# Leading the second attention with its memory heads, spreading its head transposes, preloading three activation tables, and moving late values and first output terms of the latent attention

## The chip, the cores and the metric

The kernel runs on one core of one Trainium2 chip. The metric is the device time of one execution in microseconds (us). PE is the tensor engine, ACT the scalar engine, DVE the vector engine, POOL the engine that issues some of the transfers, SP the queue that issues the weight transfers. All matrices are float32, and one product of the program is two matmul instructions in the trace (128x512: x2).

## The reference, cut to what matters

Two blocks of layers on one sequence of 256 tokens, width 1024. The change touches the second attention of the first block ("fgt") and the only latent attention of the second block ("mla"), with the start of the mixture of experts behind it.

```python
# first block, second layer: 12 heads with forgetting, 4 memory heads
s = einsum('bthd,bshd->bhts', q, k) * scale + dcum_t - dcum_s     # causal
o_mix = softmax(s) @ v
o_mem = softmax(q_mem @ k_mem.T * scale) @ v_mem                   # memory_attention
x = x + concat([o_mix, o_mem]) @ w_o
# second block, first layer: 8 heads over 512 keys (context and latent)
kv = rms_norm(c_kv) @ w_ukv                                        # keys and values
y_lat = softmax(q_l @ k_all.T * scale) @ v_all @ w_o
x = x + g1 * y_lat
# then: route each token to 2 of 32 experts; silu(x @ w_gate) * (x @ w_up) @ w_down
```

## The kernel before, in words

Each engine runs its own program, written out by hand, and waits on semaphores; the order on an engine is the order of its code. Signals are kept in stages (`st["headsB"]`, `st["fgt"]`, `st["mlaU"]`, ...); `after(engine, "fgt")` waits for all signals of a stage. PSUM has 8 banks of 128x512. Weights come through a ring of six slots (`take`, `used`), filled by SP.

The second attention. `heads("headsB", ...)` turns 56 blocks of 128 tokens so that head width lies on partitions, four blocks to a bank: memory queries (in two halves of 64 columns each, so two instructions a block), memory keys, then queries and keys of the 12 forgetting heads with 66 rows. `evac("headsB", 14)` copies the banks out, the even ones by ACT, the odd ones by DVE. Only when all are copied (`after(..., "headsB")`) does `attention("fgt")` begin, on all three engines. It runs over units, one head each: `i` goes from 0 to 18 for 16 units. In iteration `i` PE makes the scores of unit `i` (for memory heads, which are `paired`, those of `i` and `i+1` together), then `outputs(i-3)` (one group of two heads at a time), then `probs_T(i-2)` (3 or 4 transposes of the probabilities), then a `fill`, one product of the output projection `wo1` that already has its heads. DVE finds the maximum (as a minimum of the negated scores), ACT the exponential, DVE the division; ACT and DVE share the copies of transposed probabilities. The units are the 12 forgetting heads, then the 4 memory heads. `out_gemm` then makes the rest of `wo1`.

The latent attention. Before it, PE makes keys (`uk`, 8 products of two halves) and values (`uv`, 8 groups of 2 products, each waiting for the key copy of its bank); ACT scales the values into `vN`; then `attention("mla")` runs over 16 units (8 heads by 2 tiles of tokens). Beside it, `row_pair` makes rows that the next stage needs. After it, `entry` makes the output projection (`product(c, h)`, 8 products each), adds it to the tokens and prepares the routing; `route` picks experts, and `experts` runs 16 rounds of three blocks of 32 rows each. SP's `load_experts` fetches the first two experts when ring slots come free, the third after `mla_o`, and the others after `route`, each when a quarter counter of the rounds allows.

ACT loads a table when a function of another set comes: exponential after root or logarithm, silu after exponential.

Of the kernel before, what the change touches and what calls it, by code (L numbers as in the profile page):

```python
# [11 lines left out]
P = 128  # L12
KT = D // P
# [170 lines left out]
def two_blocks(nc, dram, out_x):  # L184
# [5 lines left out]
    with ctx:  # L190
# [19 lines left out]
        sum_q = sb("sum_q", [P, TC])  # L210
        gx, fgcol, gsm = (sb(n, [P, KT]) for n in ("gx", "fgcol", "gsm"))
# [128 lines left out]
        projB = area(0, TC, NH + NM, AUG)  # L340
        kvS = area(TC * (NH + NM) * AUG, TC, 2 * NH, AUG)
# [175 lines left out]
        def mla_units():  # L517

            units = []
            for h in range(MH):  # L520
# [18 lines left out]
        for i in range(12):  # L539
            FILL["fgt"][6 + i] = (i // 2, i // 2, i % 2)  # L540
# [3 lines left out]
        CONV_BANKS = 6  # L544

# [110 lines left out]
        def col(t, c, c0, n=2 * HD):  # L656
# [6 lines left out]
        HEADS_B = [(projB[:, c, NH + 2 * j, 0:HD], projB[:, c, NH + 2 * j + 1, 0:HD]) for j in range(NM // 2)  # L663
                   for c in range(TC)] + mem_k
# [3 lines left out]
        ROWS_B = [P] * 2 + [AUG] * 12  # L668

# [19 lines left out]
        def heads_out(rows, scaled):  # L689

            def at(i):
                n = rows[i]
                return (headsT[0:n, 4 * i:4 * i + 4, :], ps[0:n, i % BANKS, :].rearrange("p (a b) -> p a b", a=4),
                        -SCALE_A if i in scaled else 1.0)
            return at
# [4 lines left out]
        def shared_out(i):  # L700
            w, c = i // TC, i % TC
            if w < 3:
# [7 lines left out]
               "headsB": heads_out(ROWS_B, (0, 2, 3, 4, 5, 6, 7)),  # L710
# [141 lines left out]
        def _(pe):  # L852
# [119 lines left out]
            def heads(name, blocks, rows, after_two=None, bank0=0):  # L972

                s = st[name]
                for i in range(len(blocks) // 4):
                    bank_free(s, i)
                    if i == 2 and after_two is not None:
                        after(pe, after_two)
                    for j in range(4):
# [14 lines left out]
            def attention(name, o_name=None, beside={}):  # L994
# [4 lines left out]
                if o_name is not None:  # L999
                    order = [k for _, k, h in FILL[name].values() if h == 0]  # L1000
                    w = out_chunks(order[0], KT - 1 if KT - 1 not in order else order[-1])
# [48 lines left out]
                for i in range(n + LAG + 1):  # L1050
# [4 lines left out]
                    if name == "mla" and i in ROWS_AT:  # L1055
                        j = ROWS_AT.index(i)
                        if j:
                            g = st["g1_0"]["gate_copied"]
                            pe.wait_ge(g.sem, g.at(2 * j))
                        row_pair("g1_0", j, 6)  # L1060
# [103 lines left out]
            def entry(o_name, lhs, tag):  # L1164
                s, e, r = st[o_name], st["ent" + tag], st["route" + tag]
                w = [take().rearrange("p (k n) -> p k n", k=KT) for _ in range(2)]

                def product(c, h, between=None):
# [1970 lines left out]
```

## Time and profile before

| | before |
|---|---|
| median of 3 runs (lowest, highest) | 2126.44 us (2125.73, 2127.97) |
| the profiled execution | 2125.36 us |
| its span in the trace | 2123.5 us |
| PE busy | 1984.4 us, 93% |
| granted TensorE clock, mean | 0.978 |

The span is the profiled execution less 1.9 us around it. Times in the rows below are from the start of the span. The clock is a share of full speed: 1.00 is 2.4 GHz, 0.50 is 1.2 GHz. In brackets behind a row of the timeline stands the time the engine was idle before it and what ended that.

### The profile page before, as it was taken

The numbers are of one execution on the slowest core, as the hardware profiler recorded it, in microseconds if no ns is written. First come the engines' busy times: TensorE is split into PE (matmuls) and PEld (weight loads), VectorE is DVE, ScalarE is ACT, GpSimd is POOL, SyncE is SP. The second block draws the span as 40 slices with busy tenths as digits, with TensorE's granted clock in tenths as the row PEclk, the third lists the DMA queues.
The fourth block names the chain that finished last, engine by engine and source line by source line (L and its number), as shares of the span: only waits on it lengthen the run. The fifth ranks groups of instructions, "written<-read, shape, count | busy, mean of one in ns | idle before, by whom it ended". The sixth has DMA issues, their size and how long they took to land.

```text
span 2123.5 us, 29332 instructions
## 1 busy us (share of the span) xinstructions
PE 1984.4 (93%) x9625; PEld 1080.3 (51%) x9626; DVE 992.9 (47%) x2203; ACT 682.4 (32%) x1092; POOL 45.0 (2%) x80
## 2 busy tenths in 40 slices
PE   8999999999999999999999888889998999888887
PEld 4536777646577775554433333334774333333333
DVE  2566886303398543444444333335224444333335
ACT  1451000103400003142555444444103554444444
POOL 2000000000000000000000000001000000000000
PEclk9999999998999999999999999999999999999999
DMA  9507995433289443305899999999555999999996
GB/s 306 210 7 290 362 346 220 159 119 140 106 343 366 149 165 136 122 37 201 351 414 422 419 416 422 423 423 367 218 198 210 400 419 423 422 423 422 422 422 256
DMA packets 78655, 619.89 MB, mean 292 GB/s; under 512 B 9664, under 2 KB 10000, under 8 KB 15712
## 3 DMA queue, kind: packets, MB, share of 16 engines
q1 hardware_dynamic: 67968, 540.51, 63.4%
q0 software_dynamic: 6944, 66.35, 8.2%
q10 hardware_dynamic: 3648, 11.89, 1.4%
q8 instruction: 44, 0.72, 0.1%
q14 instruction: 51, 0.42, 0.1%
HBM read 605.08 MB, written 13.63 MB: 291 GB/s over the span
## 4 chain that ended last, share of the span: by engine, by line
PE 68%; DMA 24%; DVE 3%; ACT 2%; issue 1%; DVEq 0%; SPq 0%; ACTq 0%; POOL 0%; POOLq 0%
PE ps L856 26%; DMA big<-in_w_up 21%; PE ps L1277 14%; PE ps L1103 14%; PE ps L1115 7%; PE ps L870 2%; PE ps L1250 2%; PE ps L1279 2%; DMA big<-in_w_gate 1%; DMA big<-in_w_down 1%; ACT big L1780 1%; PE ps L1261 1%; DMA big<-in_first_final_g 0%; DMA big<-in_dense 0%; PE ps L1125 0%
## 5 line engine op out<-in xcount | busy, mean ns | idle before, releaser
L1277 PE MATMUL ps<-big,hT 128*32 128x512 f32 x3072 | 698.2, 608 | 81.8 <-ACT big L1780 66.8
L1279 PE MATMUL ps<-big,hT 128*32 x1536 | 697.0, 608 | 0.0
L1780 ACT COPY big<-big 128x1024 f32 x384 | 395.6, 1046 | 494.2 <-PE ps L1279 269.6
L2538 DVE TENSOR_SCALAR big<-big 128x1024 f32 x384 | 262.1, 692 | 437.4 <-PE ps L1279 301.7
L1277 PEld LDWEIGHTS ps<-big,hT 128*32 128x32 f32 x3072 | 189.0, 111 | 459.9 <-issue 254.3
L1103 PE MATMUL ps<-hT,big 128*128 128x256 f32 x1408 | 311.2, 379 | 0.0
L856 PE MATMUL ps<-big,hT 128*128 128x512 f32 (+4 forms) x784 | 302.1, 537 | 3.4 <-ACT hT L1719 2.1
L1103 PEld LDWEIGHTS ps<-hT,big 128*128 128x128 f32 x1408 | 266.7, 190 | 49.4 <-issue 15.2
L856 PEld LDWEIGHTS ps<-big,hT 128*128 128x128 f32 x784 | 139.2, 192 | 131.7 <-issue 123.4
L1279 PEld LDWEIGHTS ps<-big,hT 128*32 128x32 f32 x1536 | 158.3, 111 | 3.7
L1115 PE MATMUL ps<-big 128*128 128x512 f32 x352 | 159.3, 595 | 0.7 <-DVE big L2302 0.7
L856 PE MATMUL ps<-big 128*128 128x512 f32 (+15 forms) x636 | 141.0, 451 | 13.8 <-issue 5.3
L2312 DVE SCALAR_TENSOR_TENSOR big<-big,s_ccol 128x512 f32<-128x512 f32 x196 | 147.4, 752 | 7.0
L1744 ACT ACTIVATE big<-big 128x256 f32<-128x256 f32 x44 | 18.3, 417 | 367.3 <-DVE big L2294 367.3
L1250 PE MATMUL ps<-big,hT 128*96 128x512 f32 x256 | 118.1, 604 | 1.2 <-DVE hT L2504 1.2
L856 PE MATMUL ps<-hT,big 128*128 128x256 f32 (+1 forms) x480 | 113.2, 397 | 1.9 <-ACT hT L2021 1.9
L856 PEld LDWEIGHTS ps<-big 128*128 128x128 f32 (+8 forms) x636 | 69.7, 176 | 79.8 <-issue 64.3
L856 PEld LDWEIGHTS ps<-hT,big 128*128 128x128 f32 x480 | 92.3, 193 | 23.7 <-issue 11.9
L1115 PEld LDWEIGHTS ps<-big 128*128 128x128 f32 x352 | 66.1, 190 | 73.5 <-issue 69.0
L2276 DVE TENSOR_TENSOR big<-ps,big 128x512 f32<-128x512 f32 x44 | 30.4, 690 | 115.4 <-PE ps L1103 114.6
L1250 PEld LDWEIGHTS ps<-big,hT 128*96 128x96 f32 x256 | 39.3, 163 | 78.0 <-issue 76.7
L2572 DVE TENSOR_TENSOR hT<-hT,ps 96x512 f32<-96x512 f32 x32 | 21.9, 683 | 88.6 <-PE ps L1279 88.6
(331 smaller groups left out, 1258.9 us busy)
## 6 DMA issues: line engine op xcount, KB each, us to landing
big<-in_w_gate SPq DMA_DIRECT2D x128, 1024.0 KB, 23.7
big<-in_w_up SPq DMA_DIRECT2D x128, 1024.0 KB, 23.2
big<-in_w_down SPq DMA_DIRECT2D x128, 1024.0 KB, 21.7
big<-in_dense SPq DMA_DIRECT2D x52, 1536.0 KB, 8.7
big<-in_dense POOLq DMA_DIRECT2D x28, 2048.0 KB, 9.9
big<-in_dense SPq DMA_DIRECT2D x20, 2048.0 KB, 7.9
y_rows<-c_res ACTq DMA_DIRECT2D x30, 384.0 KB, 7.0
big<-in_dense SPq DMA_DIRECT2D x7, 1024.0 KB, 31.7
```

Of the source, the lines that this page charges most:

```text
L856: ins = nc.tensor.matmul(out, lhsT, rhs, start=start, stop=stop)
L870: ins = nc.tensor.transpose(out, rows, const["ident"][0:k, 0:k])
L1103: ins = nc.tensor.matmul(ps[:, t % 2, f * S:(f + 1) * S], w[:, k, f * P:(f + 1) * P], hT[:, k, S:2 * S], start=k == 0, stop=k == KT - 1)
L1115: ins = nc.tensor.matmul(ps[:, 4 + 2 * c + h, :], gT[:, t % 2, c * P:(c + 1) * P], w[:, h * BW:(h + 1) * BW], start=t == 0, stop=t == FT - 1)
L1250: ins = nc.tensor.matmul(ps[0:ROWS, h, :], onehot[:, t, :], fN[:, t, h * BW:(h + 1) * BW], start=t == 0, stop=t == T - 1)
L1277: nc.tensor.matmul(ps[g * SLOTS:(g + 1) * SLOTS, bank, :], xT[:, k, g * SLOTS:(g + 1) * SLOTS], side[:, g - 1, quarter % 2, at:at + BW], s ...
L1279: return nc.tensor.matmul(ps[0:SLOTS, bank, :], xT[:, k, 0:SLOTS], experts3[:, bass.ds(here, 1), kind * CH + row:kind * CH + row + BW] .re ...
L1780: nc.scalar.copy(side[:, 1, quarter % 2, :], experts3[:, bass.ds(there, 1), lo:lo + QW] .rearrange("p a n -> p (a n)")).then_inc(s["side2_ ...
L2276: tt(U[:, par, :, 2:S + 2], ps[:, par, :].rearrange("p (a b) -> p a b", a=2), token_scale, mult)\
L2312: ins = stt(acc, mod_w[j % 2][:, k, :], ccols[:, k, col:col + 1], acc, mult, add)
L2538: ts(side[:, 0, quarter % 2, :], experts3[:, bass.ds(there, 1), lo:lo + QW].rearrange("p a n -> p (a n)"), 1.0, None, mult).then_inc(s["si ...
L2572: tt(hm[0:ROWS, :], sgm[0:ROWS, :], ps[0:ROWS, 3, :], mult).then_inc(s["hidden_done"].sem, 1)
```

## The change

1. The second attention has its 4 memory heads first (units 0 to 3), then the 12 forgetting heads. The memory queries are kept in a packed piece `mem_q`, so that a block is turned by one instruction; for this ACT and DVE write the third and fourth bank of `b_in` in two instructions each instead of one.
2. Of the 14 banks of head transposes only the first two (memory queries and keys) are done ahead of the attention, in banks 3 and 4. The other 12 are done two at a time in iterations 0 to 5, in banks 6 and 7, queries and keys of two heads; their copies stand in the same iterations on ACT and DVE.
3. The 12 products of `wo1` in the attention stand in iterations 7 to 18 instead of 6 to 17, in the order of heads that are ready.
4. ACT runs a one-column activation (`table_for`) where a table is needed later: exponential before the first and the second attention, silu in `route`.
5. In the latent attention the values of the last four heads (4 groups) are made by PE in iteration 0, behind the first pair of scores, and scaled by ACT in iteration 1. Two products of the output projection are made in iterations 15 and 17; the wait for the end of the attention stands ahead of the last product of `product(0, 0)` instead of ahead of the first.

```diff
+        mem_q = [area((c * (NH + NM) + NH) * AUG, MEM_W) for c in range(TC)]
-               "fgt": forget_units() + mem_units(NH, F_QM, F_KM), "mla": mla_units()}
-        SLOT0 = {"nsa": 2, "fgt": 0, "mla": 0}
+               "fgt": mem_units(2, F_QM, F_KM) + forget_units(), "mla": mla_units()}
+        SLOT0 = {"nsa": 2, "fgt": 2, "mla": 0}
-            FILL["fgt"][6 + i] = (i // 2, i // 2, i % 2)
+            FILL["fgt"][7 + i] = (i // 2, (6, 7, 0, 1, 2, 3)[i // 2], i % 2)
+        V_BANKS = ((3, 4, 5, 6), (7, 3, 4, 5))
+        FIRST_BANK = {"0": 7, "1": 0}
+        TURNS_B = [0, 1] + [x for i in range(6) for x in (2 + i, 8 + i)]
+        TURN_BANK_B = [3, 4] + [6, 7] * 6
...
+            def copied_B(i):
+                e = st["headsB"]["dve_evac" if i % 2 else "act_evac"]
+                pe.wait_ge(e.sem, e.at(i // 2 + 1))
+            def turn_B(i):
+                g, bank = TURNS_B[i], TURN_BANK_B[i]
+                if i >= 4:
+                    copied_B(i - 2)
+                for j in range(4):
+                    tr(ps[0:ROWS_B[g], bank, j * P:(j + 1) * P], HEADS_B[4 * g + j],
+                       st["headsB"]["banks_ready"].sem if j == 3 else None)
...
-            heads("headsB", HEADS_B, ROWS_B, after_two="dcum")
-            after(pe, "headsB")
-            w = attention("fgt", "wo1")
+            for i in range(2):
+                turn_B(i)
+            after(pe, "dcum")
+            for i in range(2):
+                copied_B(i)
+            steps = {i: [lambda i=i: turn_B(2 * i + 2), lambda i=i: turn_B(2 * i + 3)] for i in range(6)}
+            for i in (3, 5):
+                steps[i] += [lambda i=i: copied_B(i - 1), lambda i=i: copied_B(i)]
+            steps[6] = [lambda: after(pe, "headsB")]
+            w = attention("fgt", "wo1", steps)
...
+            def late_values():
+                for c in range(4):
+                    if c:
+                        pe.wait_ge(u["uv_scaled"].sem, u["uv_scaled"].at(c))
+                    values(c, 1)
+                used()
+            for c in range(4):
+                pe.wait_ge(u["uk_scaled"].sem, u["uk_scaled"].at(c + 3))
+                values(c, 0)
+            pe.wait_ge(u["uk_scaled"].sem, u["uk_scaled"].end)
...
-            after(pe, "mlaU")
-            attention("mla")
-            after(pe, "mla")
+            attention("mla", beside={0: [late_values], 15: [lambda: early_out(0)], 17: [lambda: early_out(1)]})
+            out_done = st["mla"]["out_done"]
...
+            def table_for(function):
+                nc.scalar.activation(warm[:], const["ident"][:, 0:1], function)
...
                 nc.scalar.activation(ee, ae, ACT.Exp).then_inc(s["route_act"].sem, 1)
+                table_for(ACT.Silu)
...
             evac("mem1", TC)
-            evac("headsB", 14)
+            evac("headsB", 2)
+            attention("fgt", {i: [lambda i=i: evac("headsB", 2 * i + 4, 2 * i + 2)] for i in range(6)})
             after(act, "headsB")
-            attention("fgt")
```

PE at the head of the second attention, before: `128x128` out of `c_ident` are transposes of 128 rows, `66x128` those of the forgetting heads, the others scores.

```order
L870 MATMUL ps<-c_ident,big 64x128
L856 MATMUL ps<-c_ident,big 64x128
L870 MATMUL ps<-c_ident,big 128x128 x4
L870 MATMUL ps<-c_ident,big 66x128 x48
L856 MATMUL ps<-big 128x128
L856 MATMUL ps<-big 128x256
L856 MATMUL ps<-big 128x128
L856 MATMUL ps<-big 128x256
L856 MATMUL ps<-big 128x128
L856 MATMUL ps<-big 128x256
L870 MATMUL ps<-c_ident,big 128x128 x3
```

The same place now.

```order
L877 MATMUL ps<-c_ident,big 128x128 x8
L863 MATMUL ps<-big 128x256 x4
L877 MATMUL ps<-c_ident,big 66x128 x16
L863 MATMUL ps<-big 128x256 x4
L877 MATMUL ps<-c_ident,big 128x128 x4
L877 MATMUL ps<-c_ident,big 66x128 x8
L877 MATMUL ps<-c_ident,big 128x128 x4
L877 MATMUL ps<-c_ident,big 66x128 x8
L863 MATMUL ps<-big 128x128
L863 MATMUL ps<-big 128x256
L863 MATMUL ps<-big 64x256 x4
```

The 48 transposes of the forgetting heads stand between scores and transposes of probabilities of the memory heads, and the eight instructions on halves are gone.

ACT at the same place, before: `big<-ps 66x512` are copies of turned heads, `big,psums` the exponentials.

```order
L1937 ACT_TABLE_LOAD
L1937 ACTIVATE big<-big 128x24
L1654 ACTIVATE big<-ps,rstd_m 128x512
L1654 ACTIVATE big<-ps 128x512
L1654 ACTIVATE big<-ps 66x512 x6
L1706 ACT_TABLE_LOAD
L1706 ACTIVATE big,psums<-big,mx 128x128
```

ACT now.

```order
L1998 ACT_TABLE_LOAD
L1998 ACTIVATE big<-big 128x24
L1699 ACT_TABLE_LOAD
L1699 ACTIVATE warm<-c_ident 128x1
L1707 ACTIVATE big<-ps,rstd_m 128x512
L1707 ACTIVATE big<-ps 128x512
L1759 ACTIVATE big,psums<-ps,mx 128x256 x2
L1707 ACTIVATE big<-ps 66x512
L1759 ACTIVATE big,psums<-ps,mx 128x256 x2
L1707 ACTIVATE big<-ps 66x512
L1759 ACTIVATE big,psums<-ps,mx 128x256 x2
L1779 COPY big<-ps 128x512
```

The table load stands ahead of the copy of the memory product, and each of the six copies of turned heads stands behind an exponential.

PE from the values into the latent attention, before: `big,hT 128x512 x16` are the 8 value groups, `big 128x512` scores, `hT,c_ones` the first `row_pair`.

```order
L856 MATMUL ps<-hT,big 128x512 x16
L856 MATMUL ps<-big,hT 128x512 x16
L856 MATMUL ps<-big 128x512 x8
L856 MATMUL ps<-hT,c_ones 128x512 x2
L870 MATMUL ps<-c_ident,big 128x128 x8
```

The same place now.

```order
L863 MATMUL ps<-big,hT 128x512 x8
L863 MATMUL ps<-big 128x512 x4
L863 MATMUL ps<-big,hT 128x512 x8
L863 MATMUL ps<-big 128x512 x4
L863 MATMUL ps<-hT,c_ones 128x512 x2
```

Four value groups stand behind the first pair of scores instead of ahead of it.

PE at the end of the latent attention, before: `big 128x256` are outputs, `big,hT 128x512 x8` is `product(0, 0)` of the output projection, `128x36` the row that the routing needs.

```order
L870 MATMUL ps<-c_ident,big 128x128 x8
L856 MATMUL ps<-big 128x256 x4
L870 MATMUL ps<-c_ident,big 128x128 x8
L856 MATMUL ps<-big 128x256 x4
L856 MATMUL ps<-big,hT 128x512 x8
L856 MATMUL ps<-big,c_ones 128x36
```

The same place now.

```order
L863 MATMUL ps<-big,hT 128x512
L863 MATMUL ps<-big 128x256 x4
L877 MATMUL ps<-c_ident,big 128x128 x8
L863 MATMUL ps<-big,hT 128x512
L863 MATMUL ps<-big 128x256 x4
L863 MATMUL ps<-big,hT 128x512 x6
L863 MATMUL ps<-big,c_ones 128x36
```

Two of the eight products of the first output bank stand one ahead of each of the last two outputs.

## Rows read from the trace of the kernel before

**Rows 1.** The page, the chain that ended last: shares of the span by engine

```profile
PE 68%; DMA 24%; DVE 3%; ACT 2%; issue 1%; DVEq 0%; SPq 0%; ACTq 0%; POOL 0%; POOLq 0%
```

**Rows 2.** Windows at the first expert round: busy by engine, clock, DMA share, GB/s

```profile
1010.00:1015.00 5.00, 5.00 (x32) 2.57 (x27) 1.66 (x4) 2.03 (x2) 0.00 (x0) 0.80 0.11 18
1020.00:1025.00 5.00, 4.28 (x30) 1.80 (x24) 0.69 (x1) 2.27 (x3) 0.00 (x0) 1.00 1.01 426
```

**Rows 3.** Timeline of SP: first transfer of the fourth expert

```profile
1013.92 5.20 SPq L781 DMA_DIRECT2D big<-in_w_gate  x4
```

**Rows 4.** Chain in order of time, expert rounds: start, us, what

```profile
1127.29 23.77 DMA big<-in_w_up
```

**Rows 5.** Timeline of PE, head transposes and second attention: start, us, [idle before]

```profile
502.01 0.27 PE L870 MATMUL ps<-c_ident,big 128*64 128x128 f32 x1 [0.58 <-DVE big L2057]
...
504.35 5.89 PE L870 MATMUL ps<-c_ident,big 128*128 128x128 f32 x52
511.18 2.20 PE L856 MATMUL ps<-big 66*128 66x128 f32 x12 [0.94 <-ACT big L1654]
516.11 0.90 PE L870 MATMUL ps<-c_ident,big 128*128 128x128 f32 x3 [2.73 <-DVE big L2218]
...
553.84 10.54 PE L856 MATMUL ps<-big,hT 128*128 128x512 f32 x24 [0.56 <-ACT hT L1719]
```

**Rows 6.** Windows in the second attention, columns as in Rows 2

```profile
508.00:510.00 2.00, 2.00 (x21) 1.97 (x19) 1.63 (x3) 1.35 (x3) 0.00 (x0) 1.00 0.00 0
...
514.00:516.00 2.00, 0.00 (x0) 0.00 (x0) 0.66 (x4) 1.99 (x9) 0.00 (x0) 0.50 0.00 0
...
524.00:526.00 2.00, 1.15 (x9) 0.78 (x9) 1.96 (x11) 0.99 (x4) 0.00 (x0) 1.00 0.00 0
```

**Rows 7.** Chain in order of time, second attention in its even flow

```profile
530.61 0.87 PE ps L856 x8
531.48 0.48 PE ps L870 x3
531.95 1.52 PE ps L856 x6
```

**Rows 8.** Timeline of ACT, second attention

```profile
509.84 0.59 ACT L1654 ACTIVATE big<-ps 66x512 f32<-66x512 f32 x1 [0.28 <-PE ps L870]
512.99 1.28 ACT L1706 ACT_TABLE_LOAD   x1 [2.56 <-DVE mx L2201]
```

**Rows 9.** Timeline of DVE, second attention: copy of turned heads

```profile
510.28 0.69 DVE L2057 TENSOR_SCALAR big<-ps 66x512 f32<-66x512 f32 x1 [0.19 <-PE ps L870]
```

**Rows 10.** Timeline of ACT, first attention: exponential of a memory head's first half

```profile
89.02 0.47 ACT L1706 ACTIVATE big<-ps,mx 128x256 f32<-128x256 f32 x1
```

**Rows 11.** Timeline of DVE, first attention: maximum, reciprocal, division

```profile
90.63 0.68 DVE L2206 TENSOR_REDUCE mx<-ps 128x2 f32<-128x512 f32 x1
91.23 0.16 DVE L2214 RECIPROCAL pinv<-psums 128x2 f32<-128x2 f32 x1
91.42 0.62 DVE L2218 TENSOR_SCALAR big<-big,pinv 128x256 f32<-128x256 f32 x2
```

**Rows 12.** Timeline of PE, latent attention

```profile
884.67 13.90 PE L856 MATMUL ps<-big,hT 128*128 128x512 f32 x32
899.44 3.01 PE L856 MATMUL ps<-big 128*128 128x512 f32 x8 [0.87 <-ACT big L2003]
904.11 3.04 PE L856 MATMUL ps<-big 128*128 128x512 f32 x8 [1.66 <-ACT big L1706]
...
947.66 1.97 PE L856 MATMUL ps<-big 128*128 128x256 f32 x8 [0.83 <-ACT big L1726]
...
954.16 7.11 PE L856 MATMUL ps<-big,hT 128*128 128x512 f32 x16 [0.87 <-ACT hT L1719]
```

**Rows 13.** Timeline of DVE behind the latent attention: sum for the routing

```profile
958.76 0.66 DVE L2365 TENSOR_REDUCE big<-big 128x36 f32<-128x288 f32 x1
```

**Rows 14.** Timeline of PE, first expert round

```profile
1021.47 0.62 PE L1277 MATMUL ps<-big,hT 128*32 128x512 f32 x2 [0.72 <-ACT big L1780]
```

More of the change, by code:

```diff
@@ L970, in out_gemm, with heads @@
                 turn_of(1, 1)
-            def heads(name, blocks, rows, after_two=None, bank0=0):
+            def heads(name, blocks, rows):
                 s = st[name]
@@ L1000, in attention @@
                     order = [k for _, k, h in FILL[name].values() if h == 0]
-                    w = out_chunks(order[0], KT - 1 if KT - 1 not in order else order[-1])
+                    w = out_chunks(order[0], ([order[-1]] + [k for k in range(KT) if k not in order])[-1])
                 def fill(i):
@@ L1059, in attention @@
                             pe.wait_ge(g.sem, g.at(2 * j))
+                        else:
+                            e = st["mlaU"]["uv_scaled"]
+                            pe.wait_ge(e.sem, e.end)
                         row_pair("g1_0", j, 6)
@@ L1162, in row_pair, with entry, product @@
                     mm(ps[:, bank + h, :], const["ones"][:], d[:, 4 * h:4 * h + 4, :], True, True, s["gate_ready"].sem)
-            def entry(o_name, lhs, tag):
+            def entry(o_name, lhs, tag, w=None, begun=0, done=None):
                 s, e, r = st[o_name], st["ent" + tag], st["route" + tag]
-                w = [take().rearrange("p (k n) -> p k n", k=KT) for _ in range(2)]
-                def product(c, h, between=None):
-                    for k in range(KT):
+                if w is None:
+                    w = [take().rearrange("p (k n) -> p k n", k=KT) for _ in range(2)]
+                def product(c, h, between=None, begun=0):
+                    for k in range(begun, KT):
                         if between is not None and k == 4:
                             between()
-                        mm(ps[:, 2 * c + h, :], lhs(k, c), w[h][:, k, :], k == 0, k == KT - 1,
+                        if begun and k == KT - 1:
+                            pe.wait_ge(done.sem, done.end)
+                        mm(ps[:, FIRST_BANK[tag] if not c and not h else 2 * c + h, :], lhs(k, c), w[h][:, k, :], k == 0, k == KT - 1,
                            s["banks_ready"].sem if k == KT - 1 else None)
@@ L1646, in _, with evac @@
                     .then_inc(ident_loaded if name == "ident" else first_loaded, 16)
-            def evac(name, n):
+            def table_for(function):
+                nc.scalar.activation(warm[:], const["ident"][:, 0:1], function)
+            def evac(name, n, first=0):
                 s = st[name]
-                for i in range(0, n, 2):
+                for i in range(first, n, 2):
                     dst, src, factor = OUT[name](i)
@@ L1879, in _ @@
                 ins.then_inc(s["gelu_done"].sem, 1)
+            table_for(ACT.Exp)
             after(act, "mem0", "ropeA")
@@ L1999, in _, with values @@
             nc.scalar.copy(rkvB, ps[:, 0, :]).then_inc(q["scales_copied"].sem, 1)
-            for i in range(8):
-                c, h = i // 2, i % 2
-                act.wait_ge(u["uv_ready"].sem, u["uv_ready"].at(i + 1))
-                nc.scalar.activation(vN[:, c, h * BW:(h + 1) * BW], ps[:, (1 + i) % BANKS, :], ACT.Copy,
-                                     scale=rstd_kv[:, c:c + 1]).then_inc(u["uv_scaled"].sem, 1)
-            attention("mla")
+            def values(h):
+                for c in range(4):
+                    act.wait_ge(u["uv_ready"].sem, u["uv_ready"].at(4 * h + c + 1))
+                    nc.scalar.activation(vN[:, c, h * BW:(h + 1) * BW], ps[:, V_BANKS[h][c], :], ACT.Copy,
+                                         scale=rstd_kv[:, c:c + 1]).then_inc(u["uv_scaled"].sem, 1)
+            values(0)
+            attention("mla", {1: [lambda: values(1)]})
             after(act, "mla")
@@ L2774, in _ @@
             nc.vector.tensor_copy(kS[:, :, :, HD + 1], dc).then_inc(s["dcum_dve"].sem, 1)
-            evac("headsB", 14)
+            evac("headsB", 2)
+            attention("fgt", {i: [lambda i=i: evac("headsB", 2 * i + 4, 2 * i + 2)] for i in range(6)})
             after(v, "headsB")
-            attention("fgt")
             after(v, "fgt")
```

58 lines of the change are left out of this document (35 added, 23 removed).

## The prediction

> **What bounds the kernel now.** The chain that ended last is PE for 68% and DMA for 24% [rows 1]. Following it in order of time shows where each rules: PE down to the first expert round, then from about 1127 us on transfers of expert weights of 23 to 27 us, one round after the other [rows 4], and the same in the second set of experts. So the question for any gain ahead of the experts is whether the train of transfers starts earlier too. In the windows at the first round the transfer engines are nearly empty (share 0.11) just before the fourth expert's first transfer is issued at 1013.92, and full (426 GB/s) behind it [rows 2, 3]. That transfer waits for the routing and for the first quarters of round 0, both PE's. What PE gains before 1014 us is therefore passed on whole; what it gains inside the rounds meets a full train and is mostly lost.
>
> Next the timeline of PE where the change lies, reading the idle time in brackets. In the second attention, PE starts on the heads at 502.01; has 52 transposes in 5.89 us, 0.11 each; waits 0.94 for the last copies; makes scores from 511.18 to about 513.4; then waits 2.73 until 516.11, and the output projection's last part starts at 553.84 [rows 5]. The windows show what this wait brings: the clock is 1.00 through the transposes, 0.50 at 514 to 516, and 1.00 again at 524 [rows 6]. So PE ran at 1.2 GHz for some 10 us and was busy in it from 516.1 on: about 7.9 us that would be 4 us at 2.4 GHz.
>
> **The second attention, walked through.** Prices, all at full clock: four transposes 0.45 [rows 5]; in the even flow outputs of a pair of heads 0.87, three transposes 0.33 to 0.48, a fill with one unit's scores 1.52 [rows 7], of which the fill is 0.87 (24 instructions in 10.54, two a product [rows 5]), so scores 0.65; a pair of heads with fills 4.77 (the same outputs return at 535.38). ACT: copy of turned heads 0.59 [rows 8], exponential of a memory head two halves of 0.47 [rows 10]. DVE: maximum 0.68, reciprocal and division together about 0.75 [rows 11], copy of turned heads 0.69 [rows 9]. Scores of a pair of memory heads I take as 0.87, like the outputs, being four products on halves of the rows.
>
> PE from 502.01: 8 transposes to 502.9; it waits for both copies, DVE's last, to 503.8. Scores of units 0 and 1 to 504.7, 8 transposes to 505.6. Bank 6 comes free only when ACT has done exponential 0 (from DVE's maximum at 505.5, 0.92) and then the copy, 507.1: **a new stall of 1.5**. Behind the waiting transposes on PE are the next scores. Transposes to 508.0, scores of 2 and 3, transposes of probabilities, 8 transposes: 510.2. Then 0.15 for the division, and 0.95 for ACT's copy behind exponential 2 and a copy of probabilities: 511.75. From here DVE sets the pace. It has 0.68 + 0.75 + 0.69 an iteration and every other one a copy of probabilities of 0.69, 2.1 to 2.8 us, against PE's 2 to 3. I get the last head copies at 519.05, iteration 7's end at 521.65, four pairs of 4.77 to 540.8, and the tail of two outputs, three fills, seven transposes, 5.0, to 545.8. The output projection's last part starts at 545.8 instead of 553.84: **8.0 us less**. In it are the table load of 1.28 [rows 8], now in an idle stretch of ACT near 488 (costs nothing: the next ACT work is at 494), the four blocks turned in halves (2.4 us from 502.01 to 504.4, now 0.45), the 10 us from 504.4 in which nothing but transposes ran and then waited, the half clock, and the 0.56 ahead of 553.84, which the last fill covers.
>
> That is with the clock at 1.00 throughout. New gaps of 0.9, 1.5 and 1.1 us stand in the first 10 us, with little but transposes between. If it falls there once, for as long as before (10 us), PE does 5 us of full-clock work where the walk has 7.5 in that stretch; with a wait or two more that is 3 lost, 5.0 gained. Rows for both exist: in rows 6 the clock holds through transposes and falls in a wait of 2.73. I take 6.5, half-way, since no row decides it.
>
> The Trainium skill, "TensorE: Matmul & The Clock Gate", Part 4 (PE-mode transpose), says transposes do not count as PE being busy in the same way. The row of 508 to 510 us, nothing but transposes and clock 1.00, speaks against it. By the row the sum stays; by the rule the new head of the attention is cold from its start, which is the rival A below. The skill, "ScalarE: Activation LUTs", What ACT_TABLE_LOAD costs, gives about 2.66 us for a switch with a drain; here the load takes 1.28, ends at 514.27 [rows 8], and ACT is busy for 1.99 of the 2.00 us from 514 on [rows 6]: no drain. By the rule the sum would be 1.4 us better.
>
> **The first attention's table load** gives nothing. It stands at 87.72, but the division that needs exponential 0 starts at 91.23, behind DVE's own queue [rows 11]; 1.28 less on ACT ends there.
>
> **b_in in two instructions**: two more on ACT and on DVE, about 0.2 us each, under products of 6.9 us. Nothing.
>
> **Latent attention, start.** The 8 value groups take 13.90, 1.72 each; then stalls of 0.87 (ACT's last scaling) and 1.66 (exponential) [rows 12]. Now the four late groups, 6.9 us, stand between the first and second pair of scores, where the maximum and exponential cost PE 1.66. ACT scales a group in 0.7, so PE never waits for it, and the last is done 0.9 us after PE's, under 3.0 us of scores, ahead of the new wait at the row pair. **2.5 less.**
>
> **Latent attention, end.** Stalls of 0.83 before each of the last two outputs are filled by an early product of 0.87 each; their time is unchanged, but 1.7 us less is left behind. The stall of 0.87 ahead of 954.16 [rows 12] goes as well. PE would be done with `product(0, 0)` at about 958.3 instead of 961.1. What is late next is the routing row: DVE's sum ends at 959.42 [rows 13], and that hangs on transfers issued at the attention's end, which has not moved. So PE goes on at 959.5: **1.6 less**, not 2.6. Moving `used()` for the value weights delays one transfer by 3 us, of an expert used 100 us later: nothing.
>
> **Silu in `route`.** The load of 1.28 in round 0 makes PE wait 0.72 [rows 14], behind the train's start. 0 by the train, 0.7 in each of two layers if it counts; nearer to 0, as the transfer engines are full: 0.4 for both.
>
> Sum: 6.5 + 2.5 + 1.6 + 0.4 = 11.0. The profiled execution took 2125.36, so 2114.4; the median lies 1.1 above it: **2115.4**.
>
> **Rivals.**
> A. The clock stays low from 503 until the heads are turned. PE's work from 502.9 to the end of iteration 7 is 12 times 0.45 for heads, 0.87 twice and 0.65 four times for scores, 0.87 twice for outputs, 2.4 for probabilities and a fill of 0.87: 14.8 us at full clock, 29.5 at half. That is 532.4 instead of 521.65, so the second attention is 2.7 slower than before where the walk had 8.0 less; with the other 4.5, 2124.6. Low for half as long again as before, 2119 to 2121. For it: the gaps early, and short bursts; against it: rows 6 at 508, and that the clock came back in the kernel before after 10 us of which 8 were busy. 15% for 2118.5 to 2122.2, 5% beyond.
> B. It does not get through: the expert train has its own start. Then 2125 to 2126. Against it rows 2 and 3. 3%.
> C. Slower than before. The same clock, low on past the heads: each pair of heads then costs 4.77 more. With 1.8 left of the gain by rival A's end, it takes 1.8 + 4.3 = 6.1, more than one pair, to be 0.2% slower: low until about 544 us, 41 us in one go. Nothing in the rows of this stretch shows more than 10. 3%, at 2132 if it is low for three pairs.
> D. Better: the clock never falls there and the half clock behind the routing goes too. All of 8.0 + 2.5 + 1.6 + 1.4 is 13.5, 2113; below 2110 only with another clock gain. 4% below 2110.
>
> My forecast's own case, 2110 to 2118.5, has 70%. With rival A's nearer part the range 2110 to 2121 leaves out 4% below, 4% of rival A's nearer part and 11% beyond: 19%. A measurement of this kernel tells 0.2%, 4.3 us, from no change. Faster is all below 2122.2: 0.70 + 0.15 + 0.04 = 0.89; same takes rival A's end and B: 0.08; slower: 0.03.
>
> **What would show it.** After: the time from the first head transpose to the output projection's last part is 44 to 47 us instead of 51.8; the first exponential has no table load before it; the largest PE gap there is about 1.5, for ACT's copy behind the first exponential. PE's two stalls at the latent attention's start are gone; at its end a stall of about 1 us stands ahead of the 128x36 product, waiting for DVE. The fourth expert's transfer is issued about 11 us earlier, and the expert rounds keep their length. Wrong it would be if the clock falls at 503 to 507 and stays, if DVE's iterations take over 3 us, or if the train of transfers does not move.

## The result, and the profile after

The changed kernel takes 2115.05 us (median of 4 runs, 2111.78 to 2116.16) against 2126.96 (median of 4, 2125.73 to 2127.97): ratio 0.995, 95% interval 0.9935 to 0.9965. In a second set of runs it was 2114.79 against 2125.13, ratio 0.9946 (0.9933 to 0.996). The predicted time was 2115.4. The profiled execution took 2116.16, 9.2 less than that of before. The terms behind the sum are less well hit than the sum, as the rows and the experiments show. One run of the lead-only kernel below, 2159.07 us at a mean clock of 0.935, was in a slower state and is left out of its median and ratio.

The chain that ended last, by engine; against [rows 1], PE has two points more, the transfers one less.

```profile
PE 70%; DMA 23%; DVE 3%; ACT 2%; issue 2%; DVEq 0%; SPq 0%; POOL 0%; ACTq 0%; POOLq 0%
```

The timeline of PE through the second attention of the changed kernel: start, us, what, and in brackets the idle time before.

```profile
503.74 1.06 PE L877 MATMUL ps<-c_ident,big 128*128 128x128 f32 x8 [0.58 <-DVE big L2122]
505.89 1.14 PE L863 MATMUL ps<-big 64*128 64x256 f32 x8 [1.09 <-DVE big L2122]
506.95 1.06 PE L877 MATMUL ps<-c_ident,big 128*66 128x128 f32 x8
509.30 1.07 PE L877 MATMUL ps<-c_ident,big 128*66 128x128 f32 x8 [1.28 <-ACT big L1707]
...
514.22 1.07 PE L877 MATMUL ps<-c_ident,big 128*66 128x128 f32 x8 [0.63 <-ACT big L1707]
...
544.36 0.87 PE L863 MATMUL ps<-big 128*64 128x256 f32 x8 [0.72 <-issue]
...
548.49 3.70 PE L863 MATMUL ps<-big,hT 128*128 128x512 f32 x8
```

The last part of the output projection starts at 549.35, one product of 0.86 behind 548.49. I call the time from the first head transpose to there the stretch: 45.61 us, where [rows 5] give 51.83. The largest gap is 1.28, for ACT's copy behind the first exponential; 1.5 was forecast. The windows of [rows 6] now read:

```profile
508.00:510.00 2.00, 0.72 (x8) 0.70 (x8) 1.91 (x5) 1.87 (x8) 0.00 (x0) 1.00 0.16 68
514.00:516.00 2.00, 1.78 (x14) 1.45 (x16) 1.97 (x6) 1.66 (x6) 0.00 (x0) 1.00 0.00 0
524.00:526.00 2.00, 1.94 (x14) 1.13 (x12) 1.85 (x12) 1.08 (x5) 0.00 (x0) 1.00 0.00 0
```

The clock is 1.00 throughout, with PE busy for only 0.72 of 2.00 us in the first of them. The latent attention, against [rows 12] and [rows 13]:

```profile
881.32 7.03 PE L863 MATMUL ps<-big,hT 128*128 128x512 f32 x16
888.19 2.94 PE L863 MATMUL ps<-big 128*128 128x512 f32 x8
891.06 7.13 PE L863 MATMUL ps<-big,hT 128*128 128x512 f32 x16
898.03 2.94 PE L863 MATMUL ps<-big 128*128 128x512 f32 x8
...
946.95 5.31 PE L863 MATMUL ps<-big,hT 128*128 128x512 f32 x12
953.25 0.41 PE L863 MATMUL ps<-big,c_ones 128*128 128x36 f32 x2 [0.99 <-DVE big L2430]
```

Both stalls at its start are gone, and at its end the wait for DVE's routing row stands where it was forecast. The fourth expert's first transfer and the chain behind it, against [rows 3] and [rows 4]:

```profile
1005.58 6.14 SPq L788 DMA_DIRECT2D big<-in_w_gate  x4
```

```profile
1118.27 24.37 DMA big<-in_w_up
```

The transfer is issued 8.34 earlier, not 11 (9.69 in the second profile of the changed kernel). The account of this pair of profiles: 1.71 lost at the very start of the program, 6.22 gained in the stretch, 1.69 from there to the latent attention's first transposes of probabilities, 1.57 to the end of its output rows, 0.59 in the routing and first round. The 1.71 is a slower pass through the first products (last section), and 1 us is missing from the 1.69 for a stretch of half clock near 810 us. Between the first transfers of the two expert sets 2.36 is lost again, and behind the second set's 3.22 is gained, which makes 9.2. Over all profiles here the time between these two transfers runs from 627.1 to 631.5 us, of which the silu's early load accounts for only about 1. So a single pair can't tell terms of 1 or 2 us; the landmarks of each stage can.

### The profile page after: what moved, and what is told of

The parts are those of the page before. It is cut to its first block, busy times and chain, and to the rows that moved or that the text cites. A ratio compares the mean times of both kernels' runs of the same rounds, so it can differ in the third digit from the quotient of the medians.

```text
span 2114.3 us, 29316 instructions
## 1 busy us (share of the span) xinstructions
PE 1985.9 (94%) x9617; PEld 1080.2 (51%) x9618; DVE 992.3 (47%) x2204; ACT 682.9 (32%) x1097; POOL 45.7 (2%) x80
## 4 chain that ended last, share of the span: by engine, by line
PE 70%; DMA 23%; DVE 3%; ACT 2%; issue 2%; DVEq 0%; SPq 0%; POOL 0%; ACTq 0%; POOLq 0%
PE ps L863 26%; DMA big<-in_w_up 20%; PE ps L1302 15%; PE ps L1125 14%; PE ps L1137 7%; PE ps L877 2%; PE ps L1304 2%; PE ps L1275 2%; DMA big<-in_w_gate 1%; ACT big L1833 1%; PE ps L1286 1%; DMA big<-in_first_final_g 0%; DMA big<-in_w_down 0%; DMA big<-in_dense 0%; PE ps L1147 0%
## 5 line engine op out<-in xcount | busy, mean ns | idle before, releaser
L863 PE MATMUL ps<-big 128*128 128x512 f32 (+15 forms) x636 | 135.7, 438 | 9.5 <-issue 5.2
## 6 DMA issues: line engine op xcount, KB each, us to landing
big<-in_dense POOLq DMA_DIRECT2D x28, 2048.0 KB, 10.2
```

What stands on the lines that cost most here:

```text
L863: ins = nc.tensor.matmul(out, lhsT, rhs, start=start, stop=stop)
```

## The experiments

The table gives median and ratio to the kernel before (95% interval), from 5 rounds each (3 for the last; the first two rows are the runs of the result), and from each kernel's profile the stretch, how long the clock was 0.50 in it, and two landmarks of the latent attention: L1 from the end of the stretch to its first transposes of probabilities, L2 from there to the first transposes of the output rows. The half-clock times are read from windows of 1 us: one with a clock of 0.85 holds 0.3 us at 0.50. There is one profile of each row. The ratios are to runs of the kernel before in the same set, and not to the 2126.96: the medians of these were 2126.76 for the rows attention only, latent only and the two on the exponential, 2127.33 for lead only, products in the wait, no silu preload and two waits moved, 2125.13 for changed again, products among transposes and silu preload only, 2127.64 for the last.

| kernel | us | ratio | stretch | at 0.50 | L1 | L2 |
|---|---|---|---|---|---|---|
| before (profile above) | 2126.96 | | 51.83 | 10.2 | 355.06 | 59.30 |
| changed | 2115.05 | 0.995 (0.9935, 0.9965) | 45.61 | 0 | 353.37 | 57.73 |
| changed, again | 2114.79 | 0.9946 (0.9933, 0.996) | 45.61 | 0 | 353.40 | 57.84 |
| attention only | 2117.68 | 0.9962 (0.9948, 0.9975) | 45.61 | 0 | 355.35 | 59.30 |
| latent only | 2122.07 | 0.9975 (0.9962, 0.9987) | 54.03 | 17.1 | 352.16 | 57.70 |
| changed, no exponential preload | 2114.27 | 0.9947 (0.993, 0.9963) | 45.62 | 0 | 352.19 | 57.96 |
| before, exponential preload only | 2125.77 | 0.9995 (0.9983, 1.0007) | 51.81 | 13.7 | 355.15 | 59.30 |
| lead only | 2117.99 | 0.9966 (0.9954, 0.9979) | 49.40 | 3.4 | 352.51 | 57.79 |
| products in the wait | 2121.70 | 0.9976 (0.9964, 0.9988) | 50.55 | 3.4 | 354.89 | 59.30 |
| changed, no silu preload | 2117.02 | 0.9958 (0.9944, 0.9972) | 45.61 | 0 | 353.26 | 57.90 |
| two waits moved | 2111.03 | 0.9936 (0.9917, 0.9955) | 44.71 | 0 | 352.67 | 56.38 |
| products among transposes | 2128.54 | 1.0014 (1.0004, 1.0024) | 54.43 | 10.2 | 355.39 | 59.30 |
| silu preload only | 2123.47 | 0.999 (0.998, 0.9999) | 53.37 | 13.6 | 355.01 | 59.29 |
| turned by products | 2131.53 | 1.0023 (1.0014, 1.0033) | 57.90 | 13.7 | 354.96 | 59.30 |

**Attention only and latent only.** The diff above was split: items 1 to 3 with the second attention's `table_for`, and item 5 alone.

> The kernel before with the second attention's part alone: memory heads first, spread head transposes, packed memory queries, exponential loaded early there. Theory: the stretch from the first head transpose to the output projection's last part is 45.6 us, as in the changed kernel (51.8 before), and the gain of 6.2 passes through whole: 2120.8. Rival: part of the gain is taken back between the second attention and the experts; then the stretch is 45.6 all the same, but the time is 2122 to 2124. The latent attention's rows are as before.

> The kernel before with the latent attention's part alone: four late value groups and two early output products. Theory: from the first value product to the start of the second output product it takes 72.2 us, as in the changed kernel (76.6 before), with a wait of about 1 for DVE ahead of the 128x36 product, and 4.4 less passes through the expert train: 2122.6. Rival: the routing, where DVE is waited for, takes part of it back: the fourth expert's transfer is only 2 to 3 us earlier and the time is 2124 to 2125.

Ratios 0.9962 and 0.9975 are 8.1 us (5.3 to 11.1) and 5.3 (2.8 to 8.1) less. The stretch is 45.61 with the attention's part, but it is not "51.8 before": the latent-only kernel, whose second attention is the old one, has 54.03. Neither rival held. The latent part shortens L1 and L2 in every kernel that has it.

Why the old head differs so much from itself is in the clock. First the wait of the latent-only kernel, then its windows (of the columns, the clock is the third from the end):

```profile
517.63 0.69 PE L873 MATMUL ps<-c_ident,big 128*128 128x128 f32 x2 [2.73 <-DVE big L2247]
```

```profile
517.00:519.00 2.00, 1.37 (x6) 1.38 (x7) 1.73 (x9) 1.51 (x8) 0.00 (x0) 0.50 0.00 0
...
531.00:533.00 2.00, 2.00 (x10) 1.43 (x9) 0.57 (x5) 0.00 (x0) 0.00 (x0) 0.76 0.00 0
```

The wait is the 2.73 of [rows 5], but the clock was low for 17.1 us, to 531.9, where [rows 6] have it back at 524.

**The exponential's early load, taken away and alone.** The line is taken out of the changed kernel; the second kernel is the one before with this line put in.

```diff
             nc.scalar.activation(sgf, sgf, ACT.Ln, bias=1.0).then_inc(s["dcum_act"].sem, 1)
-            table_for(ACT.Exp)
             evac("mem1", TC)
```

> The changed kernel without the exponential's early load ahead of the second attention; 1.28 us of load stand in the first exponential of a memory head, with PE's transposes of the next heads behind it. PE's wait there, 1.28 in the changed kernel, becomes about 2.6, near the 2.73 behind which the clock was low in the kernel before. Theory one: the clock falls in a wait of that size, and costs some 3 to 4 us on top: the stretch from the first head transpose to the last part of the output projection is 50 instead of 45.6, and the time 2119.5. Theory two: only the load counts, 1.3: 46.9 and 2116.4.

> The kernel before with the exponential's early load ahead of the second attention and nothing else. PE's wait of 2.73 at the first transposes of probabilities becomes about 1.45. Theory one, the clock fell for that wait: it holds now, the stretch from the first head transpose to the last part of the output projection is 46 to 47 us instead of 51.8, and this small edit gives nearly all that the whole rebuilding of the second attention gives: 2121.5. Theory two, the clock falls all the same, for the 10 us of transposes and waits: the stretch is 50.5 and the time 2125.7.

Both theories of the first missed: nothing changed, 45.62. The timeline of ACT in that kernel shows why:

```profile
503.04 0.60 ACT L1707 ACTIVATE big<-ps 128x512 f32<-128x512 f32 x1 [7.95 <-PE ps L877]
503.66 1.28 ACT L1759 ACT_TABLE_LOAD   x1
506.39 0.47 ACT L1759 ACTIVATE big<-ps,mx 128x256 f32<-128x256 f32 x1 [1.45 <-DVE mx L2270]
```

The load runs directly behind the copy and ahead of the wait for the maximum. In [rows 8] it ran behind that wait. The order of the two programs shows the difference, the kernel before first:

```
L1706 ACT_TABLE_LOAD [waits dve_evac,max_done,act_evac]
L1706 ACTIVATE big,psums<-big,mx 128x128 [waits banks_ready]
```

```
L1759 ACT_TABLE_LOAD
L1759 ACTIVATE big,psums<-ps,mx 128x256 [waits max_done]
```

In the program with several semaphores to wait for, three of the waits stand ahead of the load; in the one that waits for the maximum alone, the load has none. So by dropping the wait for all heads the change had already hidden the load.

Alone in the old kernel, the early load cuts the wait to 1.45 and yet the stretch is 51.81:

```profile
516.42 0.90 PE L871 MATMUL ps<-c_ident,big 128*128 128x128 f32 x3 [1.45 <-DVE big L2224]
```

The clock fell at 515.2, 0.2 into the wait, and stayed low for 13.7 us. A wait half as long didn't prevent the fall: theory one falls. Theory two had the fall and the time (2125.7), but not the stretch (50.5).

**Lead without spreading, and products in the wait.** The first puts all turns ahead of the attention again (banks 6, 7, 0, 1, 2, 5 by turns); the second adds to the kernel before:

```diff
-            steps = {i: [lambda i=i: turn_B(2 * i + 2), lambda i=i: turn_B(2 * i + 3)] for i in range(6)}
...
+            for i in range(2, 14):
+                turn_B(i)
+            after(pe, "headsB")
+            w = attention("fgt", "wo1")
```

```diff
+                    if name == "fgt" and i == LAG:
+                        for _ in range(3):
+                            mm(ps[:, 6, :], const["ident"][:], w[0][:, 0, :], True, True)
```

> The changed kernel with all 14 banks of head transposes ahead of the second attention, as in the kernel before, but still led by the memory heads: the spreading undone, the lead kept. After 48 transposes in one go comes a wait of about 2.3 for the first exponential and division. In three profiles with this head (the kernel before and two experiments) the clock fell within 1 us of the end of the scores, with a wait of 2.73 or of 1.45. Theory one: the run of transposes brings the fall; the stretch from the first head transpose to the last part of the output projection is 51 to 54 us with 10 to 17 us at half clock, and the time 2121 to 2123. Theory two: the lead by memory heads is what helps; no fall, 48 us, 2117.

> The kernel before with three more products (six instructions of 128x512, results overwritten later, so no output changes) between the second scores and the first transposes of probabilities of the second attention: PE is busy through the wait of 2.73. Theory one: the wait is the trigger; the clock stays at 1.00 and the stretch is 46 to 47 us instead of 51.8 to 54, the time 2120 to 2121. Theory two: what went before the wait, 5.9 us of transposes, is the trigger; the clock falls as before, after the scores, the products take twice as long and hold up the rest by some 2 us: 54 to 56 us, 2127 to 2129.

With the lead alone, PE's timeline and the windows are:

```profile
504.09 5.41 PE L877 MATMUL ps<-c_ident,big 128*66 128x128 f32 x48 [0.87 <-DVE big L2121]
510.44 1.13 PE L863 MATMUL ps<-big 64*128 64x256 f32 x8 [0.94 <-ACT big L1706]
513.37 2.08 PE L863 MATMUL ps<-big 64*128 64x256 f32 x8 [1.80 <-ACT big L1758]
```

```profile
513.00:515.00 2.00, 1.63 (x8) 1.20 (x8) 0.78 (x3) 1.23 (x6) 0.00 (x0) 0.60 0.00 0
...
517.00:519.00 2.00, 1.31 (x10) 0.94 (x11) 1.97 (x8) 1.62 (x7) 0.00 (x0) 1.00 0.00 0
```

The clock falls, but for 3.4 us only, and the stretch of 49.40 lies between the two theories. Against it the changed kernel differs in the spreading alone and has no fall; of the 3.79 us between their stretches the 3.4 us at half clock can explain 1.7 at most, and the rest is waits that the spreading fills or removes. With the products in the wait, PE is busy from 512.29 to beyond 519, and the clock falls all the same:

```profile
512.29 2.23 PE L856 MATMUL ps<-big 66*128 66x128 f32 x12 [0.97 <-ACT big L1657]
514.33 4.43 PE L856 MATMUL ps<-big,c_ident 128*128 128x512 f32 x6
518.60 0.49 PE L870 MATMUL ps<-c_ident,big 128*128 128x128 f32 x3
```

```profile
513.00:515.00 2.00, 2.00 (x10) 1.52 (x9) 1.20 (x8) 0.90 (x1) 0.00 (x0) 0.83 0.04 8
515.00:517.00 2.00, 2.00 (x4) 0.79 (x3) 0.55 (x3) 1.99 (x8) 0.00 (x0) 0.50 0.00 0
517.00:519.00 2.00, 2.00 (x8) 0.95 (x7) 1.34 (x8) 1.24 (x6) 0.00 (x0) 0.81 0.00 0
```

So the wait of 2.73 is not what brings the fall, and theory one misses; theory two has the fall but not the 54 to 56 us. The stretch is 50.55, shorter than before although 2.6 us of useless products were added: the clock was back after 3.4 us instead of 10.2 or more. The kernel is 5.1 us faster (2.6 to 7.7), of which the stretch shows 1.3 to 3.5, by which profile of the old head it is held against.

**Is it the transposes?** Two edits to the kernel before, in `heads`: a product ahead of three of the banks, and all head blocks turned by products with the identity.

```diff
+                    if name == "headsB" and i in (4, 7, 10):
+                        mm(ps[:, i % BANKS, :], const["ident"][:], x_res[:, 0, 0:BW], True, True)
```

```diff
-                            (tr_upper if q else tr)(ps[q * m:(q + 1) * m, i % BANKS, j * P:(j + 1) * P], part,
+                            (tr_upper if q or name == "headsB" else tr)(ps[q * m:(q + 1) * m, i % BANKS, j * P:(j + 1) * P], part,
```

> The kernel before with three products more (six instructions of 128x512, overwritten later, no output changes), as in the run with products in the wait, but one each ahead of the fifth, eighth and eleventh bank of head transposes, so that the run of 48 transposes is broken into pieces; the wait of 2.73 stays as it was. Theory one: transposes alone bring the fall; here it doesn't come, the clock is 1.00 from 502 to 530 and the stretch is about 51.5 (2.6 for the products, half a clock saved), the time 2124. Theory two: the fall has to do with something else at that place (the waits, the copies, the scores on 66 rows); the clock falls as in the kernel before, the stretch is 54 to 57 and the time 2129 or more.

> The kernel before with the head blocks of the second attention turned by ordinary products with the identity (two instructions a block) instead of transposes; the order, the copies and the wait of 2.73 behind them are as they were. The rows of the old head, where a half block is turned so in 0.37 to 0.43, give 0.2 to 0.4 a block: the head takes 5 to 12 us longer. Theory one, PE's transposes do not count as work for the clock, wherever they stand: no fall, the clock is 1.00 from 502 on through the wait, and the stretch is 46 to 48 plus those 5 to 12 us. Theory two, the fall comes from something else at that place (the scores on 66 rows, the waits): the clock is 0.50 for 3 to 17 us behind the scores here too, and the stretch is 2 to 8 longer than by theory one. The whole is slower than before by either: 2127 to 2140.

Theory one missed both times. With products among the transposes the clock fell at 516.3 for 10.2 us. With no transpose in the head at all:

```profile
503.34 12.66 PE L856 MATMUL ps<-c_ident,big 128*64 128x128 f32 x120 [0.58 <-DVE big L2057]
516.93 2.20 PE L856 MATMUL ps<-big 66*128 66x128 f32 x12 [0.94 <-PE ps L856]
521.87 0.90 PE L870 MATMUL ps<-c_ident,big 128*128 128x128 f32 x3 [2.73 <-DVE big L2218]
```

```profile
519.00:521.00 2.00, 0.14 (x1) 0.00 (x0) 0.20 (x2) 1.99 (x6) 0.00 (x0) 1.00 0.00 0
521.00:523.00 2.00, 1.14 (x6) 1.14 (x7) 1.87 (x10) 1.51 (x8) 0.00 (x0) 0.61 0.00 0
```

It fell at 521.4 and was low for 13.7 us. Transposes are not needed for the fall, and in the changed kernel, where they stand between scores, there is none.

**Silu.** The changed kernel without `table_for(ACT.Silu)`, and the kernel before with it alone.

> The changed kernel without the silu's early load in the routing. Theory: PE's stall of 0.72 in the first round is back in each of the two expert sets, behind the fourth expert's first transfer, whose time of issue does not move. If the train of transfers does not care, the time is that of the changed kernel, 2115; if the train's later transfers wait for the round's quarters, 1.4 is passed on: 2116.5.

> The kernel before with the silu's early load in the routing alone. In the profiles so far the time from the fourth expert's first transfer to the first of its down weights is 19.4 us without that load and 18.4 to 18.5 with it, in both expert sets. Theory: the train of transfers starts 0.9 earlier in each set and keeps it: 1.8 less, 2125.2. Rival: it is lost behind the full transfers and the time is that of before, 2127.

Without the load taken early, PE's stall of 0.72 stands in the first round of all eight profiles (here the changed kernel without it); in the six with it there is none.

```profile
1011.48 0.62 PE L1302 MATMUL ps<-big,hT 128*32 128x512 f32 x2 [0.72 <-ACT big L1833]
```

SP's issues of the kernel with the silu preload alone:

```profile
1015.41 5.21 SPq L782 DMA_DIRECT2D big<-in_w_gate  x4
1022.27 5.23 SPq L782 DMA_DIRECT2D big<-in_w_up  x4
1033.79 6.44 SPq L782 DMA_DIRECT2D big<-in_w_down  x4
```

And of the kernel before, behind the row in [rows 3]:

```profile
1020.78 6.25 SPq L781 DMA_DIRECT2D big<-in_w_up  x4
1033.32 6.61 SPq L781 DMA_DIRECT2D big<-in_w_down  x4
```

From the first gate to the first down transfer it is 18.4; in the kernel before, 1033.32 less 1013.92, 19.4. The 1.0 arises within the second group, whose issues are spread over 6.25 us there and over 5.23 here. It shows in both expert sets. The time is 2.1 us less (0.2 to 4.3). Taken out of the changed kernel it costs 2.0 by the medians, though the intervals overlap. Both agree with the 1.8 to 2.0 by which the transfers are earlier in the two sets. The profiles say it more clearly than the medians: from the fourth expert's first transfer to the end of the span it is 1104.8 to 1108.9 us in the six with the early load (mean 1107.8) and 1109.4 to 1112.2 in the eight without it (mean 1110.6).

**Two waits moved**, on top of the changed kernel: on PE and on ACT.

```diff
                 product(0, 0, begun=begun)
+                product(0, 1)
                 pe.wait_ge(r["route_dve"].sem, r["route_dve"].at(1))
                 mm(ps[:, 3, 0:G + E], const["ones"][:], swS, True, True, r["route_pe"].sem)
-                product(0, 1)
```

```diff
-            evac("headsB", 2)
-            attention("fgt", {i: [lambda i=i: evac("headsB", 2 * i + 4, 2 * i + 2)] for i in range(6)})
+            evac("headsB", 4)
+            attention("fgt", {i: [lambda i=i: evac("headsB", 2 * i + 4, 2 * i + 2)] for i in range(1, 6)})
```

> The changed kernel with two waits moved: ACT copies the first bank of turned heads ahead of the first exponential, and PE makes the routing's 128x36 product behind the second output product. Theory: PE's wait of 1.28 for ACT shrinks to 0.1 to 0.7, of which DVE's pace leaves 0.5 us less in the stretch (45.1); the wait of 0.99 ahead of the 128x36 product is gone and the fourth expert's transfer is issued 1.5 us earlier: 2113.6. Rival: the routing's own chain on DVE takes the 1.0 back in its wait of 2.12, which grows to 3: 2114.6.

```profile
508.21 1.17 PE L877 MATMUL ps<-c_ident,big 128*66 128x128 f32 x8 [0.25 <-ACT big L1707]
...
945.30 10.03 PE L863 MATMUL ps<-big,hT 128*128 128x512 f32 x23
...
984.36 0.62 PE L863 MATMUL ps<-c_ones,big 128*32 128x128 f32 x4 [2.11 <-DVE big L2507]
```

The 1.28 became 0.25, the output products run on without a gap, and the routing's wait is 2.11 as it was 2.12: the rival falls. The stretch is 0.90 shorter and L2 1.35. The time is 2111.03, ratio to the kernel before 0.9936 (0.9917 to 0.9955). Beside the changed kernel's 2115.05 and 2114.79 that is some 4 us by the medians, but 2 to 3 by the ratios; the landmarks account for 2.3, and the rest is no larger than the scatter of the runs. It has the lowest median here, though its interval overlaps those of the changed kernel.

## Why the prediction was right, point by point

**The bound.** Gain ahead of 1014 us passes into the expert train: the attention-only kernel's stretch gained 6 to 8 and its time fell by 8.1. Right. That "what it gains inside the rounds meets a full train and is mostly lost" is the wrong part of it (silu, below).

**The second attention, 6.5.** The walk gave 8.0 at full clock; measured from the first head transpose it was 6.22, with the clock at full. The walk was 1.8 short: about 1.0 up to the end of iteration 7 (scores of a pair of memory heads are 1.14, not 0.87, the wait for DVE's copy is 1.09, not 0.9), and 0.9 in the tail, where a gap of 0.72 stands ahead of the outputs. The four pairs between cost 4.78 each, as taken. The 6.5 is half-way to a fall that didn't come, which by chance made up for what the walk had too short: the number was right for the wrong reason. The walk also names the early load of the exponential among its gains, and that gave nothing (45.62 without it): dropping the wait for all heads had hidden the load.

And 51.83 may not be what the old kernel usually spends. Three profiles with that head unchanged have 51.83, 54.03 and 53.37, mean 53.1: the same waits, but 10.2, 17.1 and 13.6 us at half clock. By their mean the change gains 7.5. The profile of before that I worked from was the most favourable of the three. Of these 7.5, the lead (53.1 to 49.40) and the spreading (49.40 to 45.61) have half each; the lead's half takes in the packed memory queries and the early load, which that kernel has too.

**The clock.** Rival A did not come in any of six profiles with the spread head. The reason I gave against it, the window of 508 to 510 at 1.00 with nothing but transposes in it, was weak: in the seven profiles with all heads turned ahead by transposes, the clock fell 3.0 to 5.2 us behind the last turn of the run, and 5.4 behind it with products for transposes, so a window at 1.00 tells little of what the work in it leads to. The Trainium skill ("TensorE: Matmul & The Clock Gate", Part 4 (PE-mode transpose)) says that transposes do not count as PE being busy in the same way. The traces do not bear that out as the cause here: the new head, with as many transposes of heads, was at 1.00 in all six profiles, and the clock fell behind the head turned by products too. What is shown is where the fall comes from: turning all heads in one run ahead of the attention, in eight of eight profiles, against none of six where the turns stand between scores. What in that run does it is open: not the wait of 2.73 behind it (products in its place), not that wait's length (1.45), not transposes. Not tested is the wait of 0.94 to 0.97 for the last copies between the run and the scores, which all eight have; waits of 1.09 and 1.28 in the new head brought no fall, but nothing like the run stands ahead of them. Also open is why the low clock lasts 3.4 us in two of them (the lead alone, and the products in the wait) and 10 to 17 in the others.

**Latent start, 2.5.** L1 is 354.9 to 355.4 without the late values, mean 355.1, and in four kernels with them 352.2 to 352.7, mean 352.4: 2.7. In the changed kernel, its repeat and the one without the silu preload it is 353.3 to 353.4; there the clock was 0.50 for some 3 us near 810, where PE waits for the last rows of the feed-forward. The forecast is right.

**Latent end, 1.6.** L2 gives 1.3 to 1.6, and the DVE wait of 0.99 stands where forecast. Right; moving the row gave 1.35 more.

**Exponential of the first attention, 0, and b_in, 0.** From the input's last transposes to the first head transpose it is 478.15 before and 478.17 after. Right.

**Silu, 0.4.** The term most off in size: 1.8 to 2.0 by the transfers and 2.1 (0.2 to 4.3) by the time. I priced PE's stall of 0.72 and called it hidden "as the transfer engines are full". But the last of the second group of transfers waits for a quarter of the round that the stall delays, and without the stall the train is 1.0 earlier in each layer. That transfers run full behind a point doesn't show that their issue isn't late.

**Sum.** 7.5, 2.7, 1.5 and 1.8 make 13.5 by the typical rows; ratios of 0.995 and 0.9946 are 10.6 (7.4 to 13.8) and 11.5 (8.5 to 14.2). The predicted 11.0 is inside, with the attention 1.0 and silu 1.4 too low in it. So the forecast lies nearer to the measured time than its own terms as measured do, and that is in part luck. The parts run alone, 8.1, 5.3 and 2.1, even make 15.5; their intervals are too wide to say whether something is lost when they stand together.

**A slip.** Rival C prices the case of three pairs at half clock at 2132. By its own terms, 4.77 a pair on top of 2124.6, that is 2138.9; 2132 belongs to a pair and a half. It has 3% and changes nothing else.

## What to carry to other kernels

Before pricing an edit where the clock is low, take two or three profiles of the same kernel: the same code gave 51.8 to 54.0 us, and a term worth 6 changes by 2 with the profile it is measured against. A table load ahead of an instruction cost time here only where waits stood ahead of the load; look whether the first user waits for one semaphore or several. And a stall inside a round whose transfers wait for its progress is priced by the issue times of those transfers, not by how full the engines are behind them.

## What the runs showed of the hardware that was not expected

The granted clock in the records doesn't tell all that slows PE. Windows of 10 to 14 us, before and then after, with the same products of 128x512 in both:

```profile
10.00:14.00 4.00, 3.98 (x10) 1.83 (x11) 0.48 (x3) 0.12 (x1) 4.00 (x8) 1.00 1.06 391
```

```profile
10.00:14.00 4.00, 4.00 (x6) 1.69 (x7) 0.48 (x3) 0.00 (x0) 4.00 (x8) 1.00 1.02 393
```

Both say 1.00, but PE gets through 10 matmuls in the one and 6 in the other, and the first 32 take 14.00 against 15.85. This is the 1.71 with which the changed kernel's profile starts behind; among the other profiles too the 32 take either 14.00 or 15.4 to 16.0, with no edit near, so it is no effect of the change. Whether it is the clock, unrecorded, or something else is open. Near 810 us the record does show the slow stretch, where the busy time does not: in the windows of 811 to 817 before and 807 to 813 after, PE is busy for the same 4.80 us, at clocks of 1.00 and 0.72, and gets through 26 matmuls in the one and 18 in the other.

```profile
811.00:817.00 6.00, 4.80 (x26) 3.41 (x25) 4.58 (x10) 5.38 (x13) 0.00 (x0) 1.00 0.97 388
```

```profile
807.00:813.00 6.00, 4.80 (x18) 3.40 (x17) 4.08 (x9) 5.35 (x12) 0.00 (x0) 0.72 0.94 380
```
